# Activations stored in reverse order along the tokens, and operands placed alike modulo 512 bytes, in a one-core decoder block

## What is computed

```python
proj = einsum('bsd,de->bse', x, w_in)         # 6656 columns: q|k|v|conv B|conv C|conv h|gate_conv|gate_attn
y_conv = cb * causal_conv3(cc * ch)           # per channel, width 3
y_attn = sliding_window_attention(q, k, v, sinks)   # 16 query heads, 4 key heads, window 128, ALiBi
merged = sigmoid(g_conv) * y_conv + sigmoid(g_attn) * y_attn
x = layer_norm(ALPHA * x + merged @ w_out)
hid = silu(x @ w_gate) * (x @ w_up)           # 2816 hidden columns
x = layer_norm(ALPHA * x + hid @ w_down)
```

## The kernel before, in words

| tensors | before | after |
|---|---|---|
| act_hi, act_lo, w_hi, w_lo, ident | 128 | 128 |
| w_hi_b, w_lo_b, m_hi, m_lo, wd_hi, wd_lo, hid_hi, hid_lo | 160 | 128 |
| q_st, ks_hi, ks_lo, pt_hi, pt_lo, prob, vs, xs, acc, sq_acc | 160 | 128 |

## Time and profile before

### The profile page before, as it was taken

How to read it: one execution, slowest core, us unless ns; L and a number is a source line. 1 busy time by engine, 2 the same in 40 slices (tenths; PEclk the granted TensorE clock), 3 DMA queues, 4 the chain that set the end, 5 groups by cost and what they waited for, 6 DMA issues and landing times.

```text
span 1526.2 us, 18733 instructions
## 1 busy us (share of the span) xinstructions
PE 1503.1 (98%) x6898; PEld 1242.3 (81%) x6898; DVE 697.7 (46%) x1063; ACT 429.9 (28%) x803; POOL 396.0 (26%) x187
## 2 busy tenths in 40 slices
PE   9999999999999999989989999999999999999997
PEld 8888888888888888868868888888888888888885
DVE  3227662766276637669677231323323132232335
ACT  3423433343334333342443111121112121111223
POOL 2121132113211321136843121302213031221303
PEclk9999999999999999999999999999999999999999
DMA  5111111111111111114332110202101020211002
GB/s 167 56 55 29 43 41 55 29 40 41 55 34 35 41 55 38 31 42 124 89 91 66 44 55 27 82 0 82 55 28 55 27 82 14 69 55 55 0 14 97
DMA packets 127754, 80.07 MB, mean 52 GB/s; under 512 B 7792, under 2 KB 122480, under 8 KB 127728
## 3 DMA queue, kind: packets, MB, share of 16 engines
q1 hardware_dynamic: 127728, 79.73, 17.4%
HBM read 75.53 MB, written 4.19 MB: 52 GB/s over the span
## 4 chain that ended last, share of the span: by engine, by line
PE 96%; DVE 3%; ACT 1%; issue 0%; POOL 0%; ACTq 0%; DVEq 0%; POOLq 0%
PE ps L975 29%; PE ps L977 29%; PE ps L976 29%; PE ps L1084 2%; PE ps L1075 2%; PE ps L1067 1%; PE ps L1066 1%; DVE act_lo L849 0%; DVE m_lo L818 0%; DVE res L868 0%; PE ps L990 0%; DVE bn L938 0%; DVE res L859 0%; DVE raw_d L952 0%; PE ps L998 0%
## 5 line engine op out<-in xcount | busy, mean ns | idle before, releaser
L975 PE MATMUL ps<-act_hi,w_hi 128*128 128x512 f32 x1184 | 463.0, 391 | 1.2 <-DVE act_lo L673 1.2
L977 PE MATMUL ps<-act_hi,w_lo 128*128 128x512 f32 x1184 | 461.7, 390 | 0.0
L976 PE MATMUL ps<-act_lo,w_hi 128*128 128x512 f32 x1184 | 461.4, 390 | 0.0
L381 POOL TENSOR_TENSOR w_lo<-raw,w_hi 128x1024 fp32r<-128x1024 f32 x54 | 131.2, 2430 | 508.4 <-ACT w_hi L468 508.4
L975 PEld LDWEIGHTS ps<-act_hi,w_hi 128*128 128x128 f32 x1184 | 222.4, 188 | 46.7 <-issue 1.4
L977 PEld LDWEIGHTS ps<-act_hi,w_lo 128*128 128x128 f32 x1184 | 222.2, 188 | 46.8
L976 PEld LDWEIGHTS ps<-act_lo,w_hi 128*128 128x128 f32 x1184 | 222.4, 188 | 45.1
L922 DVE TENSOR_TENSOR res<-res,ps 128x512 f32<-128x512 f32 x160 | 109.8, 687 | 94.1 <-PE ps L977 94.1
L401 POOL TENSOR_TENSOR w_lo_b<-raw_b,w_hi_b 128x1024 fp32r<-128x1024 f32 x22 | 52.5, 2408 | 379.2 <-ACT w_hi_b L574 379.2
L975 PE MATMUL ps<-act_hi,w_hi_b 128*128 128x512 f32 x352 | 140.7, 400 | 0.0
L977 PE MATMUL ps<-act_hi,w_lo_b 128*128 128x512 f32 x352 | 139.9, 398 | 0.0
(11 more groups left out here) (144 smaller groups left out, 1919.4 us busy)
## 6 DMA issues: line engine op xcount, KB each, us to landing
raw<-in_w_in SPq DMA_DIRECT2D x52, 512.0 KB, 3.7
raw_d<-in_w_down SPq DMA_DIRECT2D x22, 512.0 KB, 3.3
raw<-in_w_out SPq DMA_DIRECT2D x16, 512.0 KB, 3.6
raw_b<-in_w_gate SPq DMA_DIRECT2D x11, 512.0 KB, 3.8
raw_b<-in_w_up SPq DMA_DIRECT2D x11, 512.0 KB, 4.0
raw<-in_w_gate SPq DMA_DIRECT2D x11, 512.0 KB, 3.9
raw<-in_w_up SPq DMA_DIRECT2D x11, 512.0 KB, 3.9
xs<-in_x SPq DMA_DIRECT2D x8, 512.0 KB, 8.1
```

Of the source, the lines that this page charges most:

```text
L381: pool.tensor_tensor(w_lo[:, slot], raw[:, slot], fp(w_hi[:, slot]), ALU.subtract).then_inc(w_lo_s, 1)
L975: pe.matmul(bank, w_h(t), a_hi(t), start=(t == 0), stop=False)
L976: pe.matmul(bank, w_h(t), a_lo(t), start=False, stop=False)
L977: last = pe.matmul(bank, w_l(t), a_hi(t), start=False, stop=(t == tiles - 1))
```

## The change

Both activation tensors are given out as views that run backwards along the tokens, so token 0 is at the highest address, and everyone that writes or reads them steps by -1. A tensor of 480 bytes that nobody uses is put behind the permanent ones; the tensors behind it all move up by 480 bytes, which takes them from 160 to 128 modulo 512. PSUM, all other tensors' order, and the instructions and their order on every engine are the same.

```diff
-        act_hi = sb(ctx, "act_hi", [P, DT, S], F32R)
-        act_lo = sb(ctx, "act_lo", [P, DT, S], F32R)
+        act_hi = sb(ctx, "act_hi", [P, DT, S], F32R)[:, :, ::-1]
+        act_lo = sb(ctx, "act_lo", [P, DT, S], F32R)[:, :, ::-1]
         res = sb(ctx, "res", [P, DT, S])
...
         inv2 = sb(ctx, "inv2", [P, 2])
+        sb(ctx, "line_up", [P, 120])
```

## The result

The changed kernel takes 1547.13 us, the median of 4 runs (1546.88 to 1548.19), beside 1527.78 for the kernel before: a ratio of 1.0128, with a 95% interval of 1.0114 to 1.0142. It is slower by 19.4 us where 40 us less were forecast.

What follows compares the result with a forecast made beforehand. TensorE's matmul spacing was taken as the bound. Gains of 24.2, 14.0 (6.9 of them placement) and 1.9 us made 40.1 off 1527.8, so 1487.7, stated as 1487.5; range 1466 to 1549, the forecast's own 1466 to 1510.

Steps and rivals of the forecast that it cites:

- What bounds the kernel: TensorE, busy 1503.1 of 1526.2 us; the spacing of matmul starts is the cost, its excess read as two reads interfering.
- (a): Unlike operand pairs on TensorE become alike modulo 512 bytes: 6.9 us for act, 1.9 us for m, 8.8 us gained together.
- (b): Moving and stationary reads run the same way in 4608 matmuls, so meet less: act spacing falls to 219.9 ns.
- The fixed part, 3.0 ns: Part of each matmul's spacing, from transposes of 128 columns: 109.7 ns against 106.7 ns at the clock.
- Best end, 216.3 ns: Bound on direction: the two reads never meet, 56.6 us gained with m's 1.9 us, or 1471 us.
- Worst end, 439 ns: Bound on direction: backward moving operand comes only at the weights' pace, 439 ns for 512 columns, 970 us more.
- (c): Writers and readers off TensorE, 16 instructions on each of five lines: taken as 0, 11 us if backward steps doubled them.
- (d): VectorE's `prob` before TensorE turns it: 0.5 us reserve, shrinking by 0.33 us, so the cover still holds.
- Rival 3: Slower: reads in the same direction stay side by side, all 4608 matmuls take 233.2 ns; 1549 us, chance 0.14.
- Rival 1: Only placement counts, direction makes no difference to how the reads meet; 1519 us, chance 0.15.
- Rival 2: Nothing changes: the 6.5 ns have another cause than the address, as the ports are independent; 1527.8 us, chance 0.05.
- rival 4: Much slower: the moving operand cannot be fed backwards at 2.4 columns per ns; 2498 us, chance 0.10.

Runs made afterwards that it cites:

- map_both: Matmul-only kernel, no layer computed: moving and stationary pieces shifted together, then other column counts and blocks; shifts of 4 and 32 bytes gave 237.6 and 226.7 ns.
- The maps: Matmul-only kernels, no layer computed, 24 equal matmuls per line, moving piece shifted against the stationary one; forwards 226.6 to 240.0 ns, backwards least 233.3.

## Why the prediction was wrong, point by point

- **What bounds the kernel**: right. All of the change is in TensorE's spacing; its waits went from 12.9 to 11.5 us.
- **(a) Placement, 8.8 us**: right. Alone it gave 9.7 us, and m with w_hi went from 233.1 to 226.7 ns.
- **(b) Direction, "what I take"**: this is the step that failed. It put the whole excess of 10.4 ns down to the stationary read meeting the moving one, and thinned it by the ratio of speeds, 0.345, to a spacing of 219.9 ns. Measured were 233.4. It was to gain 31.3 of the 40.1 us; it cost 28.9. The first half of the step was already wrong: with 1 stationary column in place of 128, or a stationary read that never leaves one place, the excess stays. The rows of before did show that distance matters, and the load does have a part in that (226.7 and 233.4 ns at 0 and 32 bytes became 231.7 and 231.3 once the stationary read stood still); they did not show that the load causes the whole excess, and no row could tell the two apart. What the runs showed in its place is that a moving read with step -1 has 233.3 ns or more at every distance tried, with 128, 32 or 1 stationary columns.
- **The fixed part, 3.0 ns**: a slip, and no run shows it. By the rule that gave 213.3 ns for 512 columns (one a cycle of 2.4 GHz), 128 columns are 53.3 ns; 106.7 is their time at 1.2 GHz. Nor can a run of 128 columns give a fixed part, since 128 and 192 moving columns (L101, L102 of `map_both`) have the same steady spacing, 111.7 ns (from row to row it is 109.6 and 112.9, with the steps before it settled):

```profile
269.77 2.79 PE L101 MATMUL ps<-mov,wt 128*128 128x128 f32 x24
272.40 2.87 PE L102 MATMUL ps<-mov,wt 128*128 128x192 f32 x24
```

  Without the 3.0 ns the same working gives 213.3 + 0.345 x 13.4 = 217.9 ns, which is further off; the slip did not turn the sign.
- **Best end, 216.3 ns**: never reached. The least with fresh columns is 226.6 over 127 distances; with none to fetch it is 218.7.
- **Worst end, 439 ns**: wrong. A backward read holds 2.2 columns per ns (512 in 233.3 ns).
- **(c) The writers at 0**: right. The medians of the five lines are within 12 ns of the earlier trace rows.
- **(d) The softmax**: not put to the test, since TensorE became slower; the reserve at that place grew from 0.51 to 0.86 us.
- **Rival 3** named the time (1549 against 1547.1) and the spacing (233.2 against 233.4), with a chance of 0.14. Its mechanism, two reads side by side at distance 0, is not what happens: 233.3 ns stands at 55 of 127 distances, and with a stationary read that stays in one place. What carried it was the row of the unlike pair, the only other steady level that the trace had; that its number came right is luck.
- **The range**: the measured time is outside the forecast's own 1466 to 1510, and under the outer end of 1549 only because that end is rival 3's price.
- **Rival 1** is wrong in that direction counts; its time is what the padding alone gives (1519 against 1518.2). **Rival 2** falls with the padding's 9.7 us, and **rival 4** did not come.

What stays open is why a backward walk through 16-byte pieces takes longer, and why the forward walk has its good places every so many bytes. The maps give the conditions, not the circuit. A stationary read with step +1 was not run. That the cost backwards comes from travelling the same way as the weights' read is unlikely all the same: a stationary read with step 0, which travels nowhere, left it at 233.3 ns at 0, 20 and 32 bytes.

## What to carry to other kernels

Where TensorE is the bound, look at the spacing of starts in the timeline by pair of tensors, not at durations or busy shares; two levels of spacing for equal shapes point to where operands lie, and a padding of a few hundred bytes was worth 0.6% here. Stream the moving operand forwards; blocks of 128 columns in falling order, forwards inside, cost nothing in this kernel. In the map, at distance 0, such blocks of 64 went near 227 ns, blocks of 32 at 232.1 and blocks of 16 or less at 233.4. And before an excess is put down to a collision, take the suspected partner away in a small kernel: a map of 128 cases cost one run.

## What the runs showed of the hardware that was not expected

- About half of the steady spacings (63 of 127 forwards, 69 of 127 backwards) are whole multiples of 6.67 ns to within 0.15 ns, as 226.7, 233.3 and 240.0 are.
- A line settles over some matmuls, and at some distances the level it settles at depends on what ran before (20 bytes forwards: 240.0 or 235.7).
- Blocks of 16 columns turned inside, in rising order, took 266.7 ns, and 16 columns read again and again 242 ns, forwards; both are dearer than a plain backward read.
- A moving step of 2 columns took 453 ns, double.
- With 128 stationary columns, 128 and 192 moving columns cost the same 111.7 ns.
